# Output product's last piece ahead of the router's products, 1 MB sent ahead, first round gathered turned

## The reference, cut to what matters

```
x  = x + gate1 * (concat(y_s5, y_fourier) @ w_out)          # output product and residual
h2 = rms_norm(x) * (1 + scale2) + shift2
logits = h2 @ w_router + b_router                            # 1024 -> 32 experts
top 4 of 32 for each token, softmax over the 4 -> comb
for each expert e:   gate = h2 @ w_gate[e];  up = h2 @ w_up[e]          # 1024 x 1024 each
                     act  = (up + 1) * gate * sigmoid(1.702 * gate) * comb[:, e]
                     out += act @ w_down[e]
x = x + gate2 * out;  y = rms_norm(x)
```

## Time and profile before

| what | value |
|---|---|
| median of 3 runs | 1088.86 us (1088.18 to 1089.82) |
| the profiled execution's own time | 1091.33 us |
| its span, first to last instruction | 1089.5 us |
| mean granted clock of TensorE | 0.941 |
| bytes read from HBM | 443.09 MB, 408 GB/s over the span |
| PE busy / DVE / ACT / POOL | 86% / 37% / 22% / 2% |

### The profile page before, as it was taken

The page is one execution under the profiler, slowest core; times in us unless marked ns, Lnnn a source line. Parts: engine busy times, 40 slices in busy tenths (PEclk is TensorE's granted clock), DMA queues, the critical chain, the costliest instruction groups (busy, mean ns, idle before and its releaser), DMA issues.

```text
span 1089.5 us, 32878 instructions
## 1 busy us (share of the span) xinstructions
PE 934.8 (86%) x14006; PEld 564.0 (52%) x14007; DVE 403.4 (37%) x1016; ACT 243.9 (22%) x549; POOL 26.1 (2%) x34
## 2 busy tenths in 40 slices
PE   4999898999987969997878879999966999696975
PEld 2577665555553535653444455555533555353542
DVE  7999925333331313332222223333311333132323
ACT  5667524111110101110111111111100111011102
POOL 2002002000000000000000000000000000000000
PEclk9999998999998989998898999999978999898988
DMA  9759899999999999999999999999999999999995
GB/s 371 321 188 377 269 419 386 435 426 428 436 427 436 427 433 433 428 428 433 428 439 426 436 428 432 434 427 436 427 433 433 428 429 432 429 437 426 436 427 231
DMA packets 22083, 445.45 MB, mean 409 GB/s; under 512 B 2963, under 2 KB 3571, under 8 KB 5380
## 3 DMA queue, kind: packets, MB, share of 16 engines
q1 hardware_dynamic: 21348, 444.02, 96.2%
q10 hardware_dynamic: 384, 0.57, 0.1%
q0 software_dynamic: 320, 0.39, 0.1%
HBM read 443.09 MB, written 1.10 MB: 408 GB/s over the span
## 4 chain that ended last, share of the span: by engine, by line
PE 54%; DMA 35%; DVE 6%; issue 2%; ACT 1%; another core or an unknown queue 0%; SPq 0%; DVEq 0%; ACTq 0%
PE ps L1099 23%; DMA pair<-in_w_down 18%; PE ps L1133 14%; DMA pair<-in_w_up 11%; DMA pair<-in_w_gate 4%; DMA ring<-in_w_ada 3%; PE ps L1042 3%; PE ps L880 3%; PE ps L665 2%; PE ps L681 2%; PE ps L947 1%; DVE acts L1810 1%; DVE upc L1806 1%; DVE actT L1814 1%; DVE upc L1803 1%
## 5 line engine op out<-in xcount | busy, mean ns | idle before, releaser
L1099 PE MATMUL ps<-pair,XT 128*32 128x256 f32 x6528 | 402.6, 402 | 61.6 <-DMA pair<-in_w_gate 31.0
L1099 PEld LDWEIGHTS ps<-pair,XT 128*32 128x32 f32 x6528 | 222.6, 116 | 211.5 <-DMA pair<-in_w_up 34.5
L1133 PE MATMUL ps<-pair,actT 128*32 128x256 f32 x1600 | 103.5, 416 | 24.9 <-DMA pair<-in_w_down 24.0
L1471 ACT ACTIVATE sgm<-gcl 128x256 f32<-128x256 f32 x51 | 21.3, 417 | 426.7 <-DVE gcl L1801 426.7
L1803 DVE TENSOR_SCALAR upc<-ps 128x256 f32<-128x256 f32 x51 | 21.7, 425 | 229.8 <-PE ps L1099 229.8
L1133 PE MATMUL ps<-ring,actT 128*32 128x256 f32 x1664 | 95.8, 381 | 3.3 <-DMA ring<-in_w_down 1.7
L1475 ACT ACTIVATE selT<-ps 128x128 f32<-128x128 f32 x102 | 27.2, 273 | 313.6 <-PE ps L665 313.6
L1133 PEld LDWEIGHTS ps<-pair,actT 128*32 128x32 f32 x1600 | 57.3, 119 | 65.0 <-issue 36.6
L1827 DVE TENSOR_TENSOR ys<-ps,g2x 128x256 f32<-128x256 f32 x51 | 21.7, 425 | 144.0 <-PE ps L1133 144.0
L1133 PEld LDWEIGHTS ps<-ring,actT 128*32 128x32 f32 x1664 | 51.1, 110 | 41.6 <-DVE actT L1814 7.7
L1471 ACT ACT_TABLE_LOAD x50 | 64.2, 1283 | 3.8 <-issue 2.9
(11 more groups left out here) (293 smaller groups left out, 850.9 us busy)
## 6 DMA issues: line engine op xcount, KB each, us to landing
pair<-in_w_gate SPq DMA_DIRECT2D x32, 4096.0 KB, 29.7
pair<-in_w_up SPq DMA_DIRECT2D x32, 4096.0 KB, 35.2
pair<-in_w_down SPq DMA_DIRECT2D x16, 4096.0 KB, 38.6
ring<-in_w_down SPq DMA_DIRECT2D x31, 2048.0 KB, 39.0
ring<-in_w_ada SPq DMA_DIRECT2D x10, 2048.0 KB, 10.7
w<-in_w_in SPq DMA_DIRECT2D x2, 1536.0 KB, 19.6
wout<-in_w_out SPq DMA_DIRECT2D x1, 3072.0 KB, 12.5
wglu<-in_w_glu SPq DMA_DIRECT2D x1, 2304.0 KB, 11.2
```

The lines of the kernel that those rows point to most:

```text
L1099: ins = pe.matmul(out[32 * fq:32 * fq + 32, :], XT[:, k % 2, (k // 2) * 32:(k // 2) * 32 + 32], tile_of(turn, m, k)[:, fq * QU:(fq + 1) * ...
L1133: ins = pe.matmul(pY[32 * dq:32 * dq + 32, :], actT[:, k % 2, (k // 2) * 32:(k // 2) * 32 + 32], tile_of(turn, 2, k)[:, dq * QU:(dq + 1) * ...
L1471: act.activation(sgm[:, :], gcl[:, :], ACT.Sigmoid, scale=1.702).then_inc(sem("sgm_ready"), 1)
```

## The change

1. **Output product.** o[3] is made in one piece directly after o[2], ahead of all turning. Then come all the turnings (xT0, xT1, xT2), then lg0 and lg1 together, then the count of tau 0. DVE does `residual(1, 1)` and the xT2 copies before `logits(0)` and `choose(0)`. ACT squares the first half of tau 1 before it copies the turned tokens.
2. **1 MB ahead.** The last quarter of expert 1's up matrix (k 6 and 7, the second half of ring 2) is issued right after `wout`; the other 3 MB where the whole 4 MB was.
3. **First gather.** `gather_turned` writes the turned tokens straight into `pT`: tokens are stationary (128 x 128, every 2nd or 8th column) and `sel` moves (32 columns). For tau 1 `h_mid` and `rb[:, 1]` are two separate operands, summed in PSUM. `Xs`, `turn_x(0)` and their copy fall away for round 0. DVE's additions of tau 1 and the bias row come after `sel` and the counts. The gate's rows (stage g2) are made in two parts, one behind the count of tau 0, one behind the count of tau 1.
4. **SP** now waits for `gathered` 1 as well before the second half of expert 1's down matrix.

```diff
@@ SP @@
+            w_up_1 = whole(w_up[0, 1])
+            sp.dma_start(pairs[1][:, 6:8, :].rearrange("p k c -> p (k c)"), w_up_1[:, 6 * D:8 * D]).then_inc(early_in[1], 16)
...
             sp.wait_ge(bank_full, first["o3"] + 1)
-            prefetch(1, 1)
+            sp.dma_start(pairs[1][:, 0:6, :].rearrange("p k c -> p (k c)"), w_up_1[:, 0:6 * D]).then_inc(unit_in[1][1], 16)
...
             load_half(w_down[0, 1], 1, 0)
+            sp.wait_ge(sem("gathered"), 1)
             sp.wait_ge(sem("h2_ready"), 4)
             load_half(w_down[0, 1], 1, 1)
@@ PE @@
             full(project_out(o[2], 1, 0, S5_K, NCT - 1))
+            full(project_out(o[3], 1, 1, S5_K, NCT - 1))
...
+            def gather_turned(parts):
+                for x, tau, first_part, last_part in parts:
+                    for k in range(2):
+                        for kk in range(4):
+                            ins = pe.matmul(pT[:, k * P + 32 * kk:k * P + 32 * kk + 32], x(kk, k), sel[:, tau, :],
+                                            start=(first_part and k == 0 and kk == 0), stop=last_part, skip_group_check=True)
+                return ins
-            pe.wait_ge(sem("h2_ready"), 4)
-            gather(0)
+            pe.wait_ge(sem("h2_ready"), 2)
+            pe.wait_ge(sem("hr_ready"), 4)
+            pe.wait_ge(sem("sel_ready"), 1)
+            gather_turned(((lambda kk, k: h2[:, 0, kk * QU + k:(kk + 1) * QU:2], 0, True, False),))
             pe.wait_ge(sem("rounds_ready"), 1)
             b = claim(pe, "cu")
             full(pe.matmul(b[0:NE, 0:1], C("triu", slice(0, NE))[:, 0:NE], cnt[:, 1:2], start=True, stop=True))
-            turn_x(0)
+            gather_turned(((lambda kk, k: h_mid[:, 2 * kk + k::8], 1, False, False),
+                           (lambda kk, k: rb[:, 1, 2 * kk + k::8], 1, False, True))).then_inc(sem("gathered"), 1)
...
+            pe.wait_ge(early_in[1], 16 * (seen[1] + 1))
@@ ACT @@
-            empty_x(0)
-            act.wait_ge(sem("X_turned"), 1)
+            act.sem_inc(sem("Xs_ready"), 1)
+            act.sem_inc(sem("X_turned"), 1)
+            act.wait_ge(sem("gathered"), 1)
             act.copy(XT[:, :, :], pT.rearrange("p (n x) -> p n x", x=P)).then_inc(sem("XT_ready"), 1)
@@ DVE @@
             residual(1, 0, "o", 2)
-            logits(0)
-            choose(0)
             residual(1, 1, "o3")
...
             scales(1)
+            logits(0)
+            choose(0)
             logits(1)
             choose(1)
```

More of the change, by code:

```diff
@@ L1001, in _ @@
                 turn_x2(claim(pe, "xT0", i), 0, i)
[L1002 to L1007, removed]
             pe.wait_ge(sem("x2_ready"), 3)
             turn_x2(claim(pe, "xT1"), 1, 0)
[L1010 to L1018, removed]
             x2 = [claim(pe, "xT2", i) for i in range(2)]
@@ L1024, in _ @@
                 full(ins)
+            pe.wait_ge(sem("wrs_ready"), 2)
+            b = claim(pe, "lg0")
+            for i in range(2):
+                pe.wait_ge(sem("xT_ready"), 1 + i)
+                ins = logits(b, 0, range(4 * i, 4 * i + 4))
+            full(ins)
+            pe.wait_ge(sem("xT_ready"), 3)
+            b = claim(pe, "lg1")
+            logits(b, 1, range(0, 4))
             for i in range(2):
@@ L1028, in _, with gate_rows @@
             full(ins)
-            b = claim(pe, "g2")
-            for st in range(2):
+            pe.wait_ge(sem("mask_ready"), 1)
+            rk = claim(pe, "rk")
+            pe.matmul(rk[:, 0:NE], C("triu"), gt[:, 0, :], start=True, stop=True, skip_group_check=True)
+            pe.matmul(rk[:, NE:2 * NE], C("ones"), gt[:, 0, :], start=False, stop=False, skip_group_check=True)
+            pe.matmul(rk[0:NE, 64:65], gt[:, 0, :], C("ones")[:, 0:1], start=False, stop=False, skip_group_check=True)
+            def gate_rows(b, st):
                 for q in range(4):
@@ L1034, in _ @@
                                     start=True, stop=True, skip_group_check=True)
-            full(ins)
+                return ins
+            g2 = claim(pe, "g2")
+            gate_rows(g2, 0)
             def gather(r):
@@ L1056, in _ @@
             full(pe.matmul(rk[:, NE:2 * NE], C("triu"), gt[:, 1, :], start=False, stop=True, skip_group_check=True))
-            pe.wait_ge(sem("h2_ready"), 4)
-            gather(0)
+            full(gate_rows(g2, 1))
+            def gather_turned(parts):
[4 more added lines that the diff above has]
+                                            start=(first_part and k == 0 and kk == 0), stop=last_part, skip_group_check=True)
+                return ins
+            pe.wait_ge(sem("h2_ready"), 2)
+            pe.wait_ge(sem("hr_ready"), 4)
+            pe.wait_ge(sem("sel_ready"), 1)
+            gather_turned(((lambda kk, k: h2[:, 0, kk * QU + k:(kk + 1) * QU:2], 0, True, False),))
             pe.wait_ge(sem("rounds_ready"), 1)
@@ L1104, in expert_round @@
                         if bound is not None:
+                            pe.wait_ge(sem("h2_ready"), 4)
                             pe.wait_ge(sem("tables"), 1)
@@ L1422, in _ @@
                 act.mul(h_mid[:, h], h_mid[:, h], ss[:, 6:7]).then_inc(sem("hr_ready"), 1)
[L1423 to L1426, removed]
             act.wait_ge(sem("x2_ready"), 3)
@@ L1431, in _ @@
             act.activation(ss[:, 3:4], ss[:, 3:4], ACT.Identity, bias=EPS).then_inc(sem("half_squared"), 1)
+            for tau, i, stage, n in ((0, 0, "xT0", 0), (0, 1, "xT0", 1), (1, 0, "xT1", 0)):
+                b = filled(act, stage, n)
+                copy_signal(hT[:, 4 * i:4 * i + 4, tau * P:(tau + 1) * P], b.rearrange("p (k x) -> p k x", x=P),
+                            stage, n, "xT_ready")
             act.wait_ge(sem("x2_ready"), 5)
@@ L1717, in _ @@
             dve.sem_inc(sem("lmax_ready"), 1)
[L1718 to L1722, removed]
             wide = lambda a: a.broadcast_to([P, 2, NE])
@@ L1728, in bias_row @@
                     .then_inc(sem("selb_ready"), 1)
-            bias_row(0)
             b = filled(dve, "rk")
@@ L1742, in _ @@
             dve.sem_inc(sem("rounds_ready"), 1)
+            for b_ in range(2):
+                h = slice(b_ * HALF, (b_ + 1) * HALF)
+                dve.wait_ge(sem("hr_ready"), 3 + b_)
+                tt(by_k(1, b_), natural(h_mid[:, h]), natural(rb[:, 1, h]), ALU.add)
+                dve.sem_inc(sem("h2_ready"), 1)
+            bias_row(0)
             link(dve.scalar_tensor_tensor(out=rank[:, :, :], in0=b[:, 0:2 * NE].rearrange("p (t e) -> p t e", e=NE),
```

## The result

The changed kernel is slower: 1092.7 us median of 11 runs (1089.72 to 1094.4) against 1088.73 for the kernel before in the same comparison, ratio 1.0035, 95% interval 1.0025 to 1.0045, which is 2.7 to 4.9 us, 3.8 in the middle. The prediction was 2.9 us, 1091.8. The profiled span is 1091.8 us against 1089.5.

The account below looks back on a forecast made before the run. Bound by an unbroken weight stream behind 180 us; expert 2's gate matrix, issued at 200.3, lands 2.4 to 3.5 us later, taken as 2.9, added to median 1088.86: 1091.8 us. Range 1087.6 to 1094.2, the forecast's own 1090.6 to 1092.8.

Parts of the forecast that it names:

- The mark: Landing of expert 2's gate matrix (gate 2), 210.1 us before: the end moves by what it moves by.
- Parts 1 and 2: Expert 1's up matrix issued 3.5 us sooner, landing 5.3 sooner; the 1 MB's 2.4 us hidden in idle queue time.
- The way to the gather: Router's passes, masks and count ahead of the first gather: it starts at 183.2 us, 3.1 sooner than before.
- The gather: Turned first gather: 48 passes of 0.215 us at the low clock, 10.3 us against 1.97 before.
- From round 0's opening to gate 2: Round 0's opening at 194.4 us to issue of expert 2's gate matrix at 200.3: 5.9 us.
- A: Rival, faster: the clock stays at 2.4 GHz through the gather, which ends 5 us sooner; 1085.8 us; chance 0.14.
- B: Rival, no difference: gather passes cost 0.16 us at the low clock, 7.7 us in all; 1089.2 us; chance 0.20.
- C: Rival, slower still: full clock returns later in round 0, 1.7 us more, +4.6, 1093.5 us; strided loads alike; chance 0.16.
- The two costs of part 4: SP's wait alone delays landing of expert 2's gate matrix 1.3 us; PE's late freeing 2.4 to 3.5; 2.9 taken.

Follow-up runs that it names:

- c_nothing_ahead: The changed kernel without the 1 MB ahead, up 1 issued whole behind o[3]: 1093.07 us, ratio 1.0044 to the kernel before.
- f_ahead_only: The kernel before with the 1 MB ahead and nothing else of the change: 1087.97 us, ratio 1.0000 to the kernel before.
- g_order_only: The kernel before with only the new order of part 1, old first gather, no 1 MB ahead: 1085.47 us, ratio 0.9973.
- k_dense_ahead: The changed kernel with 5 unused dense products (10 passes of 416 columns) ahead of the count of tau 0: 1093.82 us, ratio 1.0051 to the kernel before.
- l_strides: k_dense_ahead with stationary strides of 4, none and 16 in the gather's three parts, so other values are gathered: one execution, 1096.83 us.
- h_pool_adds: a_old_gather with POOL instead of DVE making tau 1's two additions: 1085.69 us, ratio 0.9973 to the kernel before.
- n_32_passes_wait: b_h2_32_passes with SP's wait for the gather kept ahead of expert 1's second half down matrix: 1089.11 us, ratio 1.0006 to the kernel before.
- d_first_part_twice: The changed kernel with the turned gather's first part (tau 0, 16 passes) made twice: 1096.43 us, ratio 1.0069 to the kernel before.
- b_h2_32_passes: The changed kernel with tau 1 gathered from h2, 32 passes instead of 48, without SP's wait for the gather: 1088.74 us, ratio 1.0003 to the kernel before.
- a_old_gather: The changed kernel with the old first gather, DVE's additions ahead of sel and no SP wait for gathered: 1085.69 us, ratio 0.9977 to the kernel before.

## Why the prediction was right, point by point

**The mark.** That the end follows gate 2's landing held in all thirteen profiles, within 0.9 us of 879.4.

**Parts 1 and 2.** The last piece ended, and up 1 was issued, 4.5 us sooner in the profile; 3.5 had been worked out, and the rest is an earlier start of this execution. Both idle places closed and up 1 landed 5.9 us sooner. `x2_seeded` came in time, as worked out. That part 2 is swallowed was in the sum for the changed kernel, and c_nothing_ahead bears it out. Where the first gather is the old one it is less certain: in f_ahead_only nothing of the 1 MB shows in the time and 0.6 us in the landing, in g_order_only nothing in the time and 2.2 in the landing.

**The way to the gather.** It began 9.25 us behind up 1's issue (172.56 to 181.81), 9.7 by the sum. The prediction's own terms give a little less than it wrote: 181.45 + 1.6 is 183.05, not 183.2, and with 10.3 and 0.15 that ends 0.25 ahead of its 193.75. The count's product at the end of this way ran at the full clock still: the granted clock is 0.90 over 180 to 183, so the low level came at about 182.4. In the kernel before it came at 180.4 rather than 180.7, and the full one came back at 194.0 rather than 194.3.

**The gather.** 11.1 us against 10.45 with cu. The number is near, but the mechanism was only half of it. The sum had 48 x 0.215 at the low clock. The first 16 passes took 3.13 us (a few of them ahead of the fall), and the 32 others 7.75, 0.242 each: 0.87 us more than 0.215, and for a reason that no row of before showed, the stride of 8. There k_dense_ahead and l_strides decide: strides of 4 and 8 elements hold a load of 128 columns near 0.235 us at either clock; strides of 1 and 2 follow the clock, 0.11 to 0.12 and 0.213 to 0.22. The Trainium skill has this in "SBUF — State Buffer", under "Door 1: The DMA port swizzle": lines of 16 bytes, and two hits in each needed for full speed, and for float32 it puts the stride that is still free at 4 elements. The runs agree on the kind of rule (0.12 us with 2, 0.24 with 8, at the full clock) and differ at the edge: 4 elements, where no line is hit twice, already took 0.23. Nor does it foretell that 16 is faster than 8.

**From round 0's opening to gate 2.** 5.15 us rather than 5.9, since the clock came back sooner, about 2.4 us after the opening instead of 4.0 (the prediction has 4.3). This took back what the gather had cost too much. That the two cancel is luck: the stride's price was not in the sum, and the clock comes back at another time in each profile, from 1.4 us ahead of round 0's opening (h_pool_adds) to 4.9 us behind it (n_32_passes_wait). This execution's up 1 was issued 0.95 us ahead of the sum's 173.5; with that added, gate 2's issue is 199.7 against 200.3. Its 13.7 us to landing were a little above the 12.2 to 13.3.

**The rivals.** *A* was mispriced: a full clock would have made the gather 16 x 0.12 + 32 x 0.24, some 9.7 us, not 5.3: 1.4 us less than measured, out of a loss of 3.8. *B* is refuted by n_32_passes_wait's and d_first_part_twice's passes, 0.218 to 0.222 at the low clock with 32 moving columns, twice the 0.111 that the router's take at the full one with 64. *C* had two causes: the clock that comes back later did not come, and the strided loads did, at 0.9 us rather than C's 1.7. The middle of the measured interval, 3.8, lies a little above the 2.4 to 3.5, as this would have it; the interval's 2.7 to 4.9 do not tell it from 2.9.

**The two costs of part 4.** The prediction had SP's wait (1.3 us by itself) and PE's lateness side by side and took the later one. b_h2_32_passes and n_32_passes_wait show this to be right for 32 passes: a hole of some 2 us that the wait makes (DMA share 0.33, then 0.00 from 185 to 187 us in n_32_passes_wait) is covered by gate 2's own issue, which comes from PE. For the 48 passes it rests on the rows alone: gate 2 took 13.7 us to land, where it took 13.4 to 13.6 in the kernels a, b, f and h, which have no such wait, so the hole cost it some 0.3 us at most.

## What to carry to other kernels

Where a stream of weights sets the time and one engine must free its buffers, ask of each transfer which of two things it hangs on, bytes ahead of it or its own condition: moving bytes into idle time is worth little or nothing to a transfer that hangs on its condition. And look at what one profile says of a small gain twice, once at the moment that the edit should move and once at the clock there. Turning operands round so that the wide side is stationary saves copies and a transposition, but pays one load of 128 columns for every 32 that move; count loads, not products. And read the stride of a stationary operand as a price: with float32, 1 and 2 elements were free and 4 and 8 doubled a load at the full clock.

## What the runs showed of the hardware that was not expected

- A load of 128 x 128 float32 weights took 0.117 us with a stride of 2 elements and 0.238 with 8 at the 2.4 GHz level, and 0.238 as well at 1.2 GHz (k_dense_ahead, distances from load to load, each the part's 1.96 or 3.88 us less the last load's own time); with 16 it was 0.217 at 1.2 GHz (l_strides).
- The clock stayed at 2.4 GHz through 3.7 us of router's passes back to back (32 passes) and fell at 182.4 in the changed kernel, with the gather just begun. In the nine profiles with the same PE program up to the gather it fell 6.9 to 10.8 us behind up 1's issue; with 3.5 us of 416-column products ahead of the count, 14.0 and 16.4 us behind it (l_strides, k_dense_ahead).
- Two of DVE's steps of 32 columns, TENSOR_TENSOR and TENSOR_SCALAR, took 0.54 and 1.31 us instead of 0.19 and 0.24 while POOL added two tensors of 128 x 512; MAX8 beside them took 0.20 as without (h_pool_adds, a_old_gather).
